# A token mixer in another order: projection groups, rotary, retention heads and norms spread between the K tiles

## The reference, cut to what matters

```python
proj = x @ w_in                                  # 256 x 2048 by 2048 x 7168
sb_q, sb_k, sb_v, r_q, r_k, r_v, r_g = split(proj)    # 1024 columns each, 8 heads of 128
sb  = stick_breaking_attention(sb_q, sb_k, sb_v)      # per head: z = q k', softplus, running sums, exp, a v
sb  = sb * rsqrt(mean(sb^2) + eps) * sb_norm_w        # per head
ret = retention(rotary(r_q), rotary(r_k), r_v)        # per head: (q k' * decay) v
ret = (ret - mean) * rsqrt(var + eps) * ret_norm_w    # per head
ret = silu(r_g) * ret
mix = concat([sb, ret]) @ w_out                       # 256 x 2048 by 2048 x 2048
x   = layer_norm(alpha * x + mix)
x   = layer_norm(alpha * x + peer_ffn(x))             # routing and 16384 single-neuron experts
```

## Time and profile before

| | |
|---|---|
| time, median of 3 runs | 2142.57 us (2142.36 to 2144.0) |
| the profiled execution | 2144.47 us, its span 2142.7 us |
| mean granted clock of TensorE | 0.983 |
| busy: PE, PEld | 2061.1, 1839.6 us (96%, 86%) |
| busy: DVE, ACT, POOL | 1507.5, 1131.7, 551.4 us |
| DMA | 378.41 MB, mean 177 GB/s |

### The profile page before, as it was taken

The page is one execution under the profiler, slowest core; times in us unless marked ns, Lnnn a source line. Parts: engine busy times, 40 slices in busy tenths (PEclk is TensorE's granted clock), DMA queues, the critical chain, the costliest instruction groups (busy, mean ns, idle before and its releaser), DMA issues.

```text
span 2142.7 us, 42567 instructions
## 1 busy us (share of the span) xinstructions
PE 2061.1 (96%) x12326; PEld 1839.6 (86%) x12326; DVE 1507.5 (70%) x2372; ACT 1131.7 (53%) x1952; POOL 551.4 (26%) x380
## 2 busy tenths in 40 slices
PE   8999989897999999999999999999999999999995
PEld 6887777676889999999999999998888888888884
DVE  4556665757568889889999999965555555555556
ACT  4555445343545555456666666554555555555552
POOL 0002221101049999964444444100000000000001
PEclk9999999898999999999999999999999999999998
DMA  7675455274766666655555555557665555555552
GB/s 221 216 218 161 142 152 151 79 234 136 206 163 188 183 182 166 182 160 159 158 156 159 157 158 158 166 192 226 208 194 193 191 195 193 191 193 194 191 193 98
DMA packets 253810, 378.41 MB, mean 177 GB/s; under 512 B 41808, under 2 KB 173008, under 8 KB 253136
## 3 DMA queue, kind: packets, MB, share of 16 engines
q1 hardware_dynamic: 253776, 377.98, 58.3%
HBM read 373.69 MB, written 4.19 MB: 176 GB/s over the span
## 4 chain that ended last, share of the span: by engine, by line
PE 65%; POOL 9%; DVE 3%; issue 3%; SPq 1%; DMA 1%; ACT 0%; POOLq 0%; DVEq 0%; ACTq 0%
PE ps L382 20%; PE ps L384 20%; PE ps L383 20%; POOL split_lo L1575 8%; PE ps L626 3%; SPq L359 1%; DVE split_lo L978 1%; DMA raw<-in_w_out 0%; DMA raw<-in_expert_v 0%; DVE x_cols L1198 0%; PE ps L482 0%; DVE y_out L1204 0%; ACT split_hi L692 0%; DVE y_out L1193 0%; PE ps L377 0%
## 5 line engine op out<-in xcount | busy, mean ns | idle before, releaser
L978 DVE TENSOR_TENSOR split_lo<-raw,split_hi 128x512 fp32r<-128x512 f32 x864 | 623.4, 725 | 520.6 <-ACT split_hi L692 520.6
L692 ACT ACTIVATE split_hi<-raw 128x512 fp32r<-128x512 f32 x864 | 544.3, 631 | 610.1 <-PE ps L384 591.3
L382 PE MATMUL ps<-act_hi,split_hi 128*128 128x256 f32 x2048 | 586.0, 286 | 0.8 <-POOL split_lo L1575 0.6
L384 PE MATMUL ps<-act_hi,split_lo 128*128 128x256 f32 x2048 | 579.3, 283 | 0.0
L383 PE MATMUL ps<-act_lo,split_hi 128*128 128x256 f32 x2048 | 579.3, 283 | 0.0
L382 PE MATMUL ps<-split_hi,whalf_hi 128*128 128x512 f32 x1024 | 398.7, 389 | 3.9 <-DVE split_lo L978 3.9
L384 PE MATMUL ps<-split_hi,whalf_lo 128*128 128x512 f32 x1024 | 398.4, 389 | 0.0
L383 PE MATMUL ps<-split_lo,whalf_hi 128*128 128x512 f32 x1024 | 398.4, 389 | 0.0
L382 PEld LDWEIGHTS ps<-act_hi,split_hi 128*128 128x128 f32 x2048 | 392.6, 192 | 2.8 <-POOL split_lo L1575 2.1
L383 PEld LDWEIGHTS ps<-act_lo,split_hi 128*128 128x128 f32 x2048 | 392.8, 192 | 0.0
L384 PEld LDWEIGHTS ps<-act_hi,split_lo 128*128 128x128 f32 x2048 | 392.5, 192 | 0.0
(11 more groups left out here) (171 smaller groups left out, 2053.5 us busy)
## 6 DMA issues: line engine op xcount, KB each, us to landing
raw<-in_expert_u SPq DMA_DIRECT2D x1024, 128.0 KB, 2.9
raw<-in_expert_v SPq DMA_DIRECT2D x256, 512.0 KB, 3.7
raw<-in_w_in SPq DMA_DIRECT2D x112, 512.0 KB, 3.8
raw<-in_w_out SPq DMA_DIRECT2D x32, 512.0 KB, 4.2
raw<-in_w_pq SPq DMA_DIRECT2D x128, 128.0 KB, 2.8
cst<-in_tables SPq DMA_DIRECT2D x4, 576.0 KB, 4.7
x_nat<-in_x SPq DMA_DIRECT2D x4, 512.0 KB, 7.5
x_dram<-x_cols SPq DMA_DIRECT2D x1, 2048.0 KB, 7.9
```

Source lines behind the costliest of these rows:

```text
L382: nc.tensor.matmul(acc, l_hi, r_hi, start=first, stop=False)
L384: return nc.tensor.matmul(acc, l_lo, r_hi, start=False, stop=last)
L692: nc.scalar.activation(split_hi[:, q % SPLITS, :], raw[:, q // 2, q % 2, :], ACT.Copy).then_inc(hi_ready, 1)
L978: vec.tensor_tensor(split_lo[:, q % SPLITS, :], raw[:, q // 2, q % 2, :], split_hi[:, q % SPLITS, :].bitcast(f32), ALU.subtract).then_inc( ...
```

## The change

The order of the groups: four groups first (first halves of attention queries, keys and values, and of retention queries), then the four second halves, then groups 8 to 13 as before. Attention heads run in the fifth to the twelfth group of this order (`SB_AT = 4`) in place of the seventh to the fourteenth. The tables come in three pieces in place of four, each ahead of a group in place of behind one, and the norm weights after the fourth group.

Rotary: the same products, but each waits until a certain tile of the current group has been split (`in_tile`, tiles 3, 6, 9 and 13); a token block takes one group, so that it covers the ninth to the twelfth group.

Retention heads: all eight run between K tiles of the thirteenth and fourteenth group, a head every two tiles, in one set of PSUM banks; ScalarE copies query and key together in place of ScalarE and VectorE half each. `sb_norm` becomes 16 products of 128 columns, each of which scales and weights at once. The transposes of the attention half stand after tiles 24 to 27 of the 32 (`AT_MIX0`), those of the retention half after tiles 11 to 14 of the first 16 output tiles (`AT_MIX1`). The retention norm starts in the last four tiles of the projection and ends in the first output tiles. The silu is cut in two, after output tiles 4 and 6 on ScalarE, and GpSimd's two gate products follow it.

```diff
-TABLE_PIECES, PIECE = 4, 1152
-SB_GROUP = 3 * SBH * HD // COLS
+TABLE_PIECES, PIECE = 3, 1536
+SB_AT = 4
+RT_AT = SB_AT + SBH
-RT_FIRST = 7
+AT_MIX0, AT_MIX1 = 24, 11
@@ block.sync
-            with sp.Fori(1, TABLE_PIECES + 1) as g:
-                dense(w_in_v, 0, g, True)
+            with sp.Fori(1, SB_AT) as g:
                 piece = bass.ds(g * PIECE - PIECE, PIECE)
                 sp.dma_start(cst[:, piece], tables[:, piece]).then_inc(tab_in, 16)
+                dense(w_in_v, 0, g, True, g * (2 * COLS))
...
-            with sp.Fori(TABLE_PIECES + 1, G_IN) as g:
+            with sp.Fori(SB_AT, 2 * SB_AT) as g:
+                dense(w_in_v, 0, g, True, g * (2 * COLS) - 7 * COLS)
+            with sp.Fori(2 * SB_AT, G_IN) as g:
                 dense(w_in_v, 0, g, True)
@@ block.tensor
+            def rt_heads(first):
+                def after(k):
+                    n, it = first + k, (first + k) // 2
+                    if n % 2 == 0:
+                        if 0 <= it - 2 < RTH:
+                            values(it - 2)
+                        if 0 <= it - 1 < RTH:
+                            z_product(it - 1)
+                        if it < RTH:
+                            turn_qk(it)
+                    if 0 <= n - AT_MIX0 < 4:
+                        turn_mixed(0, n - AT_MIX0)
+                return after
+
+            for s in range(2):
+                dense(RT_AT + s, s, rt_heads(s * KT))
...
-            turn_mixed(0)
-            out_half(0, 0, last_heads)
-            turn_mixed(1)
+            def second_mix(n):
+                if 0 <= n - AT_MIX1 < 4:
+                    turn_mixed(1, n - AT_MIX1)
+
+            pe.wait_ge(turn_done, F_MIX + 4)
+            out_half(0, 0, second_mix)
+            pe.wait_ge(turn_done, F_MIX + 8)
             out_half(0, 1)
@@ block.scalar
             for n in range(4, 20):
                 split(Q_OUT + n // 8 * 8, n % 8)
...
+                if n == 4:
+                    act.wait_ge(acc_free, G_IN + 2)
+                    nc.scalar.activation(proj[:, 0, gate_cols], proj[:, 0, gate_cols], ACT.Silu).then_inc(gated, 1)
+                if n == 6:
+                    nc.scalar.activation(proj[:, 1, gate_cols], proj[:, 1, gate_cols], ACT.Silu).then_inc(gated, 1)
+                if 0 <= n - 4 - AT_MIX1 < 4:
+                    mixed_hi(1, n - 4 - AT_MIX1)
@@ block.vector
+            def sb_norm(b, h):
+
                 dve.wait_ge(rstd_ready, 1)
+                r, cols = RSTD + SBH * b + h, slice(h * HD, h * HD + HD)
+                vec.scalar_tensor_tensor(out=mixed[:, b, cols], in0=mixed[:, b, cols], scalar=stats[:, r:r + 1],
+                                         in1=norm_w[:, cols], op0=ALU.mult, op1=ALU.mult).then_inc(sb_ready, 1)
...
+            def rt_heads(first):
+                def after(q):
+                    n, it = first + q - 4, (first + q - 4) // 2
+                    if n == 0:
+                        sb_variances()
+                    if n % 2 == 0 and 0 <= it - 1 < RTH:
+                        decayed(it - 1)
+                    if n % 2 == 1 and 1 <= it <= SBH:
+                        for m in (2 * it - 2, 2 * it - 1):
+                            sb_norm(m // SBH, m % SBH)
+                    if n % 2 == 0 and 0 <= it - 3 < RTH:
+                        head_stats(it - 3)
+                    if n == AT_MIX0 - 2:
+                        head_variances()
+                    if 0 <= n - AT_MIX0 < 4:
+                        mixed_lo(0, n - AT_MIX0)
+                    if n >= AT_MIX0 + 4:
+                        norm_step(n - AT_MIX0 - 4)
+                return after
...
+                if n - 4 < NORM_STEPS - 2 - in_pair:
+                    norm_step(n - 4 + in_pair)
+                if n in (9, 11):
+                    norm_step(NORM_STEPS - 2 + (n - 9) // 2)
@@ block.gpsimd
+            def in_tile(g, k):
+
+                pool.wait_ge(lo_ready, g * KT + k)
+
+            def rotary(kind, b, g):
...
+                in_tile(g, 3)
+                chain.add(eng.tensor_tensor(rot[:, 1, :, 0:half], xs[:, :, half:HD],
+                                            sin_t[:, b:b + 1, 0:half].to_broadcast([P, RTH, half]), ALU.mult))
+                in_tile(g, 6)
...
+                in_tile(g, 9)
...
+                in_tile(g, 13)
+                eng.tensor_tensor(xs, rot[:, 0, :, :], rot[:, 1, :, :], ALU.add).then_inc(rot_ready, 1)
...
-                if n == 0:
-                    pool.wait_ge(gated, 1)
+                if n == 1:
                     pool.wait_ge(norms_in, 32)
                     for b in range(TB):
+                        pool.wait_ge(gated, b + 1)
```

More of the change, by code:

```diff
@@ L257, in _, with dense @@
         def _(sp):
-            def dense(view, first_q, g, wait):
+            def dense(view, first_q, g, wait, col=None):
                 for kk in range(KT // 2):
@@ L505, in turn_mixed @@
[L505 to L511, removed]
+                pe.wait_ge(o_out, SBH + it)
+                nc.tensor.matmul(ps[:, 7, 0:P], soft_a[:, p, 0:P], proj[:, 0, v], start=True, stop=True)
@@ new lines, in values, with turn_mixed @@
+                nc.tensor.matmul(ps[:, 7, P:256], soft_a[:, p, P:256], proj[:, 0, v], start=True, stop=False)
+                nc.tensor.matmul(ps[:, 7, P:256], soft_a[:, p, 256:384], proj[:, 1, v], start=False, stop=True
+                                 ).then_inc(o_ready, 1)
+            def turn_mixed(kind, f):
+                b, col = f // 2, (kind * HALF + f % 2 * 4) * P
+                pe.wait_ge(sb_ready, (b + 1) * SBH) if kind == 0 else pe.wait_ge(mixed_ready, b + 1)
+                turn(F_MIX + 4 * kind + f, [mixed[:, b, col + i * P:col + (i + 1) * P] for i in range(4)])
@@ L1097, in head_variances @@
                 dve.wait_ge(v_chain, chain.n)
-                for it in range(RT_FIRST, RTH):
+                for it in range(RTH):
                     head_moments(it)
@@ L1106, in norm_step @@
             def norm_step(step):
-                b, part = step // 5, step % 5
+                b, part = (step // 4, step % 4) if step < TB * 4 else (step - TB * 4, 4)
                 if part < 4:
@@ L1133, in _, with mixed_lo @@
-            mixed_lo(0)
-            dve.wait_ge(v_chain, chain.n)
-            for it in range(RT_FIRST):
-                head_moments(it)
+            def mixed_lo(kind, f):
+                dve.wait_ge(turn_hi, HALF + 4 * kind + f + 1)
+                k = kind * HALF + f % 2 * 4
+                part = act_hi[:, k:k + 4, f // 2 * P:(f // 2 + 1) * P]
+                vec.tensor_tensor(act_lo[:, k:k + 4, f // 2 * P:(f // 2 + 1) * P],
+                                  ps[:, 4 + f, :].rearrange("p (k t) -> p k t", k=4), part.bitcast(f32),
+                                  ALU.subtract).then_inc(turn_done, 1)
@@ L1148, in _ @@
-                if it > RTH + 3 and it - RTH - 4 < NORM_STEPS:
-                    norm_step(it - RTH - 4)
-            for step in range(20 - 4 + RT_FIRST - RTH - 4, NORM_STEPS):
-                norm_step(step)
-            mixed_lo(1)
+                if n - 4 < NORM_STEPS - 2 - in_pair:
+                    norm_step(n - 4 + in_pair)
+                if n in (9, 11):
+                    norm_step(NORM_STEPS - 2 + (n - 9) // 2)
+                if 0 <= n - 4 - AT_MIX1 < 4:
+                    mixed_lo(1, n - 4 - AT_MIX1)
@@ L1541, in _ @@
-            with pool.Fori(5, SBH) as i:
-                stage_head(i)
+            pool.wait_ge(acc_free, q_at + 2)
+            rotary(0, 0, q_at)
+            stage_head(5)
+            rotary(0, 1, q_at + 1)
+            stage_head(6)
+            pool.wait_ge(acc_free, k_at + 2)
+            rotary(1, 0, k_at)
+            stage_head(7)
+            rotary(1, 1, k_at + 1)
             def norm_last(n, buf, w, b_, done):
```

211 lines of the change are left out of this document (67 added, 144 removed).

## The result

The changed kernel takes 2101.33 us (2100.92 to 2102.96), the kernel before 2142.47 in the same comparison: ratio 0.9814, 95% interval 0.9803 to 0.9826. That is 41.1 us less, against 37.7 forecast (2104.9; range 2101 to 2112). Measured once more, beside some of the variants, it took 2104.38, ratio 0.9822 (0.9806 to 0.9839).

A forecast was written before the change was run, and what follows sets the result against it. TensorE bounds the kernel, so only its stands and slow clock can be gained. Up to the second output pair 40.8 us gained, less 2.6 (gate) and 0.5 (rotary): 37.7, from 2142.57 to 2104.9 us; range 2101 to 2112.

The forecast's parts named there:

- Order of groups: Projection groups reordered, tables and norm weights sent earlier: bounds 0 to 1 us of cost, taken as 0.
- Rotary: Spacing GpSimd's rotary products over four projection groups: gain 18.7 us, cost taken as 0.5 us in all.
- zero slack: Before an attention head's sums (line 431): second softmax step ends right when the sums' weights load, at 187.31.
- Retention heads: Heads between tiles of the last two projection groups: 14.1 + 0.4 + 1.8 = 16.3 us added, no hand-over waits expected.
- The serial stage and first half: Serial retention stage goes; first 16 output tiles take 23.9 us in place of 30.4, plus 2.6 for the gate.
- The hand-over at its end: Last hand-over in the first output half: 2.1 us of ScalarE and VectorE steps against 1.8 of TensorE work; 0.3 us.
- The gate: GpSimd's gate products beside early output tiles hold VectorE and make TensorE stand: 2.6 us, bounds 0 to 4.5.
- Rival A: Gate products hide because their starts fall where VectorE has a lead; 2102.3 us, chance 0.16.
- Second half: Second half of the first output pair: 1.9 us of slow clock go, wait for output weights stays; 23.9 us.
- the wait for output weights: Before the second output pair: weights queued behind the same 3 MB of keys and norm weights; 2.09 us wait stays.
- The rest: Everything after the first output pair (routing, experts), from 450 us on: not touched, its time taken as unchanged.
- the sign that the prediction had named: The forecast as a whole is wrong if anything after 450 us changes its length.

The follow-up runs named there:

- heads alone: Changed kernel with retention heads and first transposes taken out from between tiles and run after the two dense groups; 2115.55 us, ratio 0.9875.
- packed again: Changed kernel with the spacing waits of the rotary products removed, so GpSimd runs them back to back; 2120.58 us, ratio 0.9904.
- spaced in the kernel before: Kernel before with only the rotary products spaced over groups 8 to 11, in the old group order; 2124.16 us, ratio 0.9915.
- one product late: Changed kernel with the third rotary product waiting for 11 split tiles of its group in place of 9; 2113.77 us, ratio 0.9863.
- a head at every tile: Changed kernel with a retention head at every K tile in place of every second; 2103.69 us, ratio 0.9824.

## Why the prediction was right, point by point

**Order of groups (0).** Right. Plain groups 21.76, the first attention group 24.60, no wait in between. Two of the runs show the order by itself: with the rotary spaced and no retention head in the projection, it takes 344.81 - 39.08 = 305.7 us from the first copy to the last in the new order (heads alone) and 345.61 - 39.83 = 305.8 in the old one.

**Rotary (18.7 gained, 0.5 paid).** The mechanism is shown by three runs (packed again, spaced in the kernel before, one product late). The term was off by 0.6: 215.8 - 197.0 = 18.8 gained, nothing paid. I had let the spaced product run for the 2.85 us of the earlier trace rows; on its own it takes 2.4, so it and the splits behind it end before the softmax steps. The zero slack was real: two tiles later it costs 1.7 us a group.

**Retention heads (16.3 added).** Measured 16.3, as a sum; its terms (14.1, 0.4 and 1.8) were not measured apart. No hand-over was waited for, and half the distance would do.

**The serial stage and first half (30.0 and 30.4 become 23.9 + 2.6).** The stage is gone. The first half takes 386.75 - 359.74 = 27.0 us (359.74 is the copy at 360.47 less the 0.73 between TensorE's end and that copy before); forecast 26.5. The hand-over at its end cost 0.28, forecast 0.3. The gate cost 2.7 to 2.9, forecast 2.6, in stands of 0.82 and 1.52 us, where 1 to 2.5 each were named. Here the size has some luck in it: the steps as the prediction lists them end at 10.6 for a tile wanted at 8.2, a stall of 2.4, and nothing in it gives its 2.5 to 2.9. The prediction let the split of tile 6 wait for the second product; in the trace it is the norm step ahead of that split which is held, and the split follows it. The time is nearly the same. Rival A (the products hide) is out by the stands in the trace, not by the time: its 2102.3 is nearer to the measured 2101.33 than the forecast's 2104.9.

**Second half (23.9).** Measured 409.51 - 386.75 = 22.8. No slow clock, as forecast, but the reason given for it (TensorE no longer stands ahead of this half) isn't shown: the spaced kernel before has the same stands and no slow clock either. Here the step failed that kept the wait for output weights at its 2.1 us: it was 0.7 in this execution, 0.8 in the next, up to 3.9 in variants. With the 2 MB of norm weights moved away the wait is gone, so they cause it; how long it is varies between profiles, and one profile does not fix it. This is 1.1 of the 1.3 us by which the forecast (37.7) missed what was gained up to the second pair (39.0); the rotary gave 0.6 more than forecast, and the first half took 0.5 more.

**The rest.** The forecast took what follows 450 us as unchanged. It was 2.8 us shorter in the first profile and 1.0 shorter in the second, with no instruction moved. Read strictly, this is the sign that the prediction had named for the forecast as a whole being wrong. It is within the spread of the runs: over the eight profiles of either order with full clock at that point this part takes 1689.0 to 1692.7 us, and the kernel before ranged from 2138.2 to 2146.0 over all comparisons. An effect of the change on it isn't shown. That 2101.33 still fell into the range, 0.3 us above its lower end, is in part luck: the second measurement, 2104.38, is within 0.6 us of the forecast.

The Trainium skill, "SBUF — State Buffer", section "Who interferes with whom", gives the lock between VectorE and GpSimd as its single rule. The traces agree where both engines read two large operands (2.54 us for a split beside a gate product, 0.69 alone). They disagree for GpSimd's powers, beside which a split keeps its 0.69 us (last section). And the runs show what it means here: removing no collision but placing each one where VectorE has a lead was worth 18.8 us.

## What to carry to other kernels

Work of GpSimd that collides with VectorE need not be made smaller to be free: ask of each piece which step of VectorE it will hold, and how far ahead of TensorE that step is. The same 2.4 us product was free behind one tile and cost 1.7 us two tiles later. A serial chain of small steps between engines costs a busy TensorE only its own instructions if it is cut into steps between dense tiles; one tile of 1.36 us was enough cover for each hand-over. And what is moved has to be priced again at its new neighbours: the gate products cost 5.2 us beside the retention heads, 2.7 to 2.9 between two output tiles, and some 0.7 in pieces.

## What the runs showed of the hardware that was not expected

- A VectorE norm step of two 128-column instructions with one tensor operand each (the other operands are columns of scalars) was held by a GpSimd product too: 2.65 us for both, 0.60 when the products are left out. Small and single-operand did not mean free.
- GpSimd's power of 16 columns takes 3.2 to 3.3 us but holds almost nothing: a split inside it took 0.69 us.

```profile
304.71 3.21 POOL L1555 TENSOR_TENSOR stats<-stats 128x16 f32<-128x16 f32 x1 [11.58 <-DVE stats L1051]
...
305.42 0.69 DVE L974 TENSOR_TENSOR split_lo<-raw,split_hi 128x512 fp32r<-128x512 f32 x1 [0.28 <-ACT split_hi L681]
```

  Two splits in a row at the start of the second power (348.41 us) took 1.52 us, against 1.28 elsewhere.
- Spaced, the rotary products of GpSimd are shorter themselves: 2.41 and 1.30 us for 1024 and 512 columns, against 2.85 and 1.74 when packed beside VectorE.
- Stands of up to 2.23 us, a third of a 26 us stretch in all, left the granted clock at 1.00. Behind longer single stands the next 4 us had a clock of 0.50 (2.80 us, late product), 0.57 (2.90, spaced kernel before) and 0.58 (3.86, heads alone), but of 1.00 behind 3.00 (a head at every tile) and 3.44 (packed again); behind the 5.79 us of the earlier trace rows it was 0.50 for 5 us. Two short stands close together, 0.94 and 1.90 us in the kernel before, were followed by 0.71 there and by 1.00 in the spaced kernel before. So the length of a stand alone doesn't tell what the clock does behind it.
